# Post-norm, residual update and next pre-norm done by halves of the tokens, in a two-layer DeltaNet / RWKV-7 decoder step

## The chip, the cores and the metric

The kernel runs on one core of one Trainium2 chip. The metric is device time in microseconds (us) for one execution, as the median of three runs. TensorE is called PE here, VectorE DVE, ScalarE ACT, GpSimd POOL and the queue of SyncE, which issues all transfers, SP.

## The reference, cut to what matters

Two layers process 512 prompt tokens and 32 sample tokens (544 in all, width 1024). Each layer is a feed-forward block, a mixer, and a second feed-forward block, each of them between two RMS norms:

```
h = h + 0.5 * rms_norm(swiglu(rms_norm(h, ng[0]), w_in, w_out), ng[1])
u = rms_norm(h, ng[2])
out = gdn_mixer(u, ...)  if i % 2 == 0 else rwkv_mixer(u, ...)
h = h + rms_norm(out, ng[3])
h = h + 0.5 * rms_norm(swiglu(rms_norm(h, ng[4]), w_in2, w_out2), ng[5])
```

So six products end in a post-norm (norms 1, 3, 5, 7, 9, 11), and five of these are followed at once by the pre-norm of the next block (norms 2, 4, 6, 8, 10).

## The kernel before

Activations lie transposed: the 1024 features are 8 tiles `m` of 128 partitions, and each tile has 2 halves of `HALF` = 272 tokens. The residual is `h`, with row `2*m + half` of the tile. Products are done in fp32 precision by three matmuls of a split operand: weights are `whi + wlo`, activations `xh + xl` (or `mh + ml` inside a feed-forward block), and one product step is `xh*whi`, `xl*whi`, `xh*wlo`, each 128x128 weights by 272 tokens. A unit is one column tile of weights: `unit_mm` (L318) runs half 0 over all 8 row tiles (11 for the feed-forward outputs, which have two units per column tile), then half 1, and raises `acc` after each half. SP loads weights into four `raw` slots, ACT copies a slot to `whi` (`split_hi`, L277, and `early_hi`, L288), and POOL subtracts for `wlo` (`split_lo`, L302, and `early_lo`, L294).

At the end of an output product (`ffn0_out`, `gdn_out`, `ffn1_out`, `ffn2_out`, `wo`, `ffn3_out`) this happens for each column tile: ACT copies it to `y` with the norm's gain (L567) and squares it to `tb` (L570), and DVE adds up the squares in `tb[2]` (L587). During the last unit ACT already splits the first three units of the next product (`early_hi`, two into buffers of their own, the third into `whi`). After the last tile, `norm_pe` sums squares over the partitions with matmuls of a 128x32 block of ones (`quarter_sums`, L388, four blocks of 136 tokens), ACT takes the root (`norm_act`, L423), ACT splits unit 3 of the next product (`early_hi(..., 3)`, L288, with POOL's L294 behind it), DVE takes the reciprocal (`root_dve`, L431), and PE spreads the result to all partitions with an identity column (`spread_norm_pe`, L414).

Then `post_norm_dve` goes through the 8 tiles, whole tiles of 544 tokens: `tb[3] = y * row` (L476), `h += step * tb[3]` (L480), with the low part of the tile before, `xl = h*gain - xh` (`pre_norm_low`, L465), in between. ACT follows with `xh = h*gain` (L451) and the square (L455). PE takes each tile as it comes (`behind_norm_tiles`): units 0 and 1 in both halves, unit 2 in half 0 alone (its other half lies in a PSUM bank that holds the post-norm's row), and between unit 0 and unit 1 the tile's sum of squares for the pre-norm (`square_sum_pe`, L388). The products are L350 to L352. After the last tile come the other half of unit 2 (`behind_norm_half`), the spread of the pre-norm's root, and unit 3. The pre-norm's root scales the products afterwards, so PE doesn't wait for it before the first products.

Before norm 8 (`lora`) DVE also scales two weight tiles (`lora_scale_dve`), and ACT splits both unit 2 and unit 3 there after the root. All queues are written out by hand in program order, with semaphores between them. After the last block DVE updates 8 tiles, and SP stores two tiles at a time (`yT`).

Of the kernel before, what the change touches and what calls it, by code (L numbers as in the profile page):

```python
# [22 lines left out]
P = 128  # L23
# [45 lines left out]
for _name, _units, _kt in PRODUCTS:  # L69
# [10 lines left out]
SETS = {n: i for i, n in enumerate(  # L80
    ["ffn0_in", "gdn_in", "gdn_out", "ffn1_in", "ffn2_in", "lora", "x0", "x1", "x2", "wo", "ffn3_in"])}
# [47 lines left out]
def trunk_kernel(nc, a):  # L129

    es = ExitStack()
    with es:
# [185 lines left out]
        def unit_mm(pe, name, u, j, out, hi, lo, k0=0, start=True, stop=True, ready=None):  # L318
# [5 lines left out]
            for half in range(2):  # L324
                for k in range(kt):
                    if ready is not None and half == 0:
                        pe.wait_ge(x_lo, ready + k + 1)
                    wh = whi[two][:, k * P:(k + 1) * P]
                    wl = wlo[two][:, k * P:(k + 1) * P]
                    r = 2 * (k0 + k) + half  # L330
                    o = out[:, half, :]
                    pe.matmul(o, wh, hi[:, r, :], start=(start and k == 0), stop=False)  # L332
                    pe.matmul(o, wh, lo[:, r, :], start=False, stop=False)  # L333
                    mm = pe.matmul(o, wl, hi[:, r, :], start=False, stop=(stop and k == kt - 1))  # L334
                mm.then_inc(acc, 1)

        def first_units_mm(pe, name, sett):
# [3 lines left out]
            for k in range(NM):  # L341
                pe.wait_ge(x_lo, 8 * sett + k + 1)
# [13 lines left out]
        def behind_norm_mm(pe, name, q):  # L356
            behind_norm_tiles(pe, name, q)
            behind_norm_half(pe, name)
# [3 lines left out]
        def behind_norm_tiles(pe, name, q):  # L362
# [3 lines left out]
            for k in range(NM):  # L366
                pe.wait_ge(x_lo, 8 * SETS[name] + k + 1)
                for j in range(3):
                    if k == 0:
                        pe.wait_ge(w_lo, base + j + 1)  # L370
                    if j == 1:
                        square_sum_pe(pe, q, k)
                    first_products(pe, j, k, *bufs[j], halves=(0, 1) if j < 2 else (0,))
            if q:
                pe.wait_ge(h_upd, 8 * (q // 2))

        def behind_norm_half(pe, name):
            two = BASE[name] % 2
            for k in range(NM):
                first_products(pe, 2, k, whi[two], wlo[two], halves=(1,))  # L380


        QT = T // 4

        def quarter_sums(pe, bank, t, first, last):

            for qd in range(4):
                mm = pe.matmul(ps[32 * qd:32 * qd + 32, bank, HALF:HALF + QT], M["ones"][:, 0:32],  # L388
                               t[:, qd // 2, QT * (qd % 2):QT * (qd % 2) + QT], start=first, stop=last)
            return mm  # L390

        def post_rows():
            return ps[:, 5:7, 0:HALF]
# [4 lines left out]
        def square_sum_pe(pe, q, m):  # L398
            pe.wait_ge(sq_ready, 8 * q + m + 1)
            mm = quarter_sums(pe, norm_bank(q), tb[m % 2], m == 0, m == NM - 1)  # L400
            mm.then_inc(sq_added, 1)

        def post_sums_pe(pe, q):
            pe.wait_ge(sq_added, 8 * q + 7)
            pe.wait_ge(sq_ready, 8 * q + 8)
            quarter_sums(pe, norm_bank(q), tb[2], True, False)
            quarter_sums(pe, norm_bank(q), tb[1], False, True).then_inc(sq_added, 1)

        def spread_norm_pe(pe, q):

            pe.wait_ge(rs_ready, q + 1)
            for qd in range(4):
                o = ps[:, qd, HALF:HALF + QT] if q % 2 == 0 else post_rows()[:, qd // 2, QT * (qd % 2):QT * (qd % 2) + QT]
                mm = pe.matmul(o, M["ident"][:, 32 * qd:32 * qd + 1].broadcast_to([P, P]), rs[:, 0, 0:QT], start=True, stop=True)  # L414
            mm.then_inc(nrm_mm, 1)

        def norm_pe(pe, q):
            post_sums_pe(pe, q)
            spread_norm_pe(pe, q)

        def norm_act(act, q):
            act.wait_ge(sq_added, 8 * (q + 1))
            act.activation(rs[:, 0, 0:QT], ps[:, norm_bank(q), HALF:HALF + QT], ACT.Sqrt, bias=eps[:, 0:1], scale=1.0 / D).then_inc(rt_ready, 1)  # L423

        def norm_copy_act(act, q):
            act.wait_ge(nrm_mm, q + 1)
            act.activation(flat(rs).rearrange("p (q t) -> p q t", q=4), ps[:, 0:4, HALF:HALF + QT], ACT.Copy).then_inc(rs_full, 1)

        def root_dve(dve, q):
            dve.wait_ge(rt_ready, q + 1)  # L430
            dve.reciprocal(rs[:, 0, 0:QT], rs[:, 0, 0:QT]).then_inc(rs_ready, 1)  # L431

# [4 lines left out]
        def clear_squares(dve, q):  # L437

            dve.wait_ge(nrm_mm, q)
# [3 lines left out]
        def pre_norm_act(act, q, sett):  # L443

            for m in range(NM):
                if q:
                    act.wait_ge(h_upd, 8 * (q // 2 - 1) + m + 1)
                elif m % 2 == 0:
                    act.wait_ge(h_in[m // 2], 16)
                if sett is not None:  # L450
                    act.activation(xh[:, 2 * m:2 * m + 2, :], h[:, 2 * m:2 * m + 2, :], ACT.Copy,  # L451
                                   scale=v(V_NORM + q * NM + m)).then_inc(x_hi, 1)
                if 8 * q + m - 1 > 0:
                    act.wait_ge(sq_added, 8 * q + m - 1)
                act.activation(tb[m % 2][:, :, :], h[:, 2 * m:2 * m + 2, :], ACT.Square).then_inc(sq_ready, 1)  # L455
                if q == 0 and m == 5:
                    early_hi(act, "ffn0_in", 3)
            norm_act(act, q)
            if sett is None:
                norm_copy_act(act, q)  # L460

        def pre_norm_low(dve, q, sett, m):

            dve.wait_ge(x_hi, 8 * sett + m + 1)
            dve.scalar_tensor_tensor(xl[:, 2 * m:2 * m + 2, :], h[:, 2 * m:2 * m + 2, :], v(V_NORM + q * NM + m),  # L465
                                     xh[:, 2 * m:2 * m + 2, :].bitcast(F32), ALU.mult, ALU.subtract).then_inc(x_lo, 1)

        def post_norm_dve(dve, q, step, sett=None, y=y):

            root_dve(dve, q)  # L470
            dve.wait_ge(nrm_mm, q + 1)
            base = 8 * (q // 2)
            for m in range(NM):
                if base + m > 0:
                    dve.wait_ge(h_upd, base + m)
                dve.tensor_tensor(tb[3][:, :, :], y[:, 2 * m:2 * m + 2, :], post_rows(), ALU.mult).then_inc(h_tmp, 1)  # L476
                if sett is not None and m:
                    pre_norm_low(dve, q + 1, sett, m - 1)
                dve.wait_ge(h_tmp, base + m + 1)
                dve.scalar_tensor_tensor(h[:, 2 * m:2 * m + 2, :], tb[3][:, :, :], step,  # L480
                                         h[:, 2 * m:2 * m + 2, :], ALU.mult, ALU.add).then_inc(h_upd, 1)
            if sett is not None:
                pre_norm_low(dve, q + 1, sett, NM - 1)


        def ffn_pe(pe, f):
# [11 lines left out]
            def out_body(i, first):  # L498
                for j in range(4):
                    m2 = j // 2  # L500
                    if j % 2 == 0 and not first:
                        pe.wait_ge(sq_ready, 8 * q + 2 * i + m2 - 1)
# [4 lines left out]
                    unit_mm(pe, name, i * 4, j, pair(m2), mh, ml, k0=KTO * (j % 2), start=(j % 2 == 0), stop=(j % 2 == 1))  # L507
            out_body(0, True)
            with pe.Fori(1, 4) as i:
                out_body(i, False)  # L510
# [34 lines left out]
        def out_act(act, name, per_tile, q, then, y=y, begun=False, ahead=0):  # L545
# [6 lines left out]
            def body(i, last):  # L552
                for j in range(4):
# [8 lines left out]
                    if j % per_tile == per_tile - 1:  # L562
                        mt = j // per_tile
                        m = (4 // per_tile) * i + mt
                        act.wait_ge(acc, 2 * (n + 1))

                        act.activation(y[:, ds(2 * m, 2), :], pair(mt), ACT.Copy, scale=vec[:, ds(V_NORM + q * NM + m, 1)])  # L567
                        if not isinstance(i, int) or i or mt >= 2:
                            act.wait_ge(sq_added, 8 * q + m - 1)
# [9 lines left out]
        def out_dve(dve, name, per_tile, q):  # L579
            clear_squares(dve, q)  # L580

            def body(i, last):
                for mt in range(4 // per_tile - last):
                    m = (4 // per_tile) * i + mt
                    dve.wait_ge(sq_ready, 8 * q + m + 1)
                    dve.wait_ge(sq_added, 8 * q + m)
# [2438 lines left out]
```

## Time and profile before

| | |
|---|---|
| runs | 2829.35, 2828.2, 2829.18 us; median 2829.18 us |
| profiled execution | span of 2825.6 us from its first to its last instruction; the record gives no separate time for it, the median is 3.6 us above this span |
| busy | PE 93%, DVE 40%, POOL 37%, ACT 31% |
| mean granted PE clock | 0.962 of 2.4 GHz |
| chain that ended last | PE, nearly throughout |
| DMA | 202.8 MB, 72 GB/s mean |

How to read it: an engine's busy time is the union of its instructions; matmuls are pipelined, so the start of one and the start of the next give what one costs PE, and its own duration (0.29 us for a product of 272 tokens at full clock) is longer than that. A bracket behind a row tells how long the engine was idle before it, and what ended the idle time.

### The profile page before, as it was taken

What the parts mean: (1) busy time and instruction counts of PE and PEld (TensorE: products, weight loads), DVE (VectorE), ACT (ScalarE), POOL (GpSimd) and SP (SyncE); (2) the same over time, 40 slices, a digit from 0 to 9 for tenths busy, and PEclk for the clock granted to TensorE, in tenths of its full rate; (3) what the DMA queues carried; (4) which work ended last, traced back from release to release, by engine and by line L of the source; (5) the groups of instructions that cost most, each with busy time, mean ns of one, the idle gap of its engine ahead of it and who ended that gap; (6) DMA issues with size and microseconds to landing.
All of it is one profiled execution on the core that took longest, in us unless ns stands there. A gap on an engine that the chain in (4) does not pass through costs nothing. (4 is left out here: it accounts for less than half of the span.)

```text
span 2825.6 us, 61605 instructions
## 1 busy us (share of the span) xinstructions
PE 2623.7 (93%) x26993; PEld 2540.6 (90%) x26993; DVE 1124.5 (40%) x1382; ACT 880.2 (31%) x1223; POOL 1056.0 (37%) x495
## 2 busy tenths in 40 slices
PE   7999998997999999999999999799588888999997
PEld 7999998996888899999899999799377858999997
DVE  3333117845544433321433311631654454433312
ACT  4222223233323422222322222333523333322221
POOL 3444442333434344443344443133034353244432
PEclk9999999998998999999999999899789999999999
DMA  4223221221012222322222222122000022122221
GB/s 149 82 89 99 92 74 60 87 67 38 2 61 105 68 89 82 94 93 81 62 88 89 92 92 85 32 89 73 19 3 3 4 81 81 53 89 89 99 88 46
DMA packets 53585, 202.82 MB, mean 72 GB/s; under 512 B 6320, under 2 KB 6448, under 8 KB 53424
## 3 DMA queue, kind: packets, MB, share of 16 engines
q1 hardware_dynamic: 53424, 200.38, 21.7%
q8 instruction: 137, 2.24, 0.3%
q14 instruction: 24, 0.20, 0.0%
HBM read 190.68 MB, written 9.67 MB: 71 GB/s over the span
## 5 line engine op out<-in xcount | busy, mean ns | idle before, releaser
L302 POOL TENSOR_TENSOR wlo<-raw,whi 128x1024 fp32r<-128x1024 f32 (+1 forms) x261 | 708.8, 2716 | 1124.8 <-ACT whi L277 1124.8
L332 PE MATMUL ps<-xh,whi 128*128 128x272 f32 x3600 | 1039.5, 289 | 6.6 <-POOL wlo L302 3.2
L334 PE MATMUL ps<-xh,wlo 128*128 128x272 f32 x3600 | 1043.5, 290 | 0.0
L333 PE MATMUL ps<-xl,whi 128*128 128x272 f32 x3600 | 1036.0, 288 | 0.0
L332 PEld LDWEIGHTS ps<-xh,whi 128*128 128x128 f32 x3600 | 678.6, 189 | 9.8 <-issue 5.8
L333 PEld LDWEIGHTS ps<-xl,whi 128*128 128x128 f32 x3600 | 679.5, 189 | 0.0
L334 PEld LDWEIGHTS ps<-xh,wlo 128*128 128x128 f32 x3600 | 677.4, 188 | 0.0
L277 ACT ACTIVATE whi<-raw 128x1024 fp32r<-128x1024 f32 (+1 forms) x261 | 297.7, 1140 | 1128.3 <-PE ps L334 1108.4
L334 PE MATMUL ps<-mh,wlo 128*128 128x272 f32 x1408 | 406.1, 288 | 0.0
L333 PE MATMUL ps<-ml,whi 128*128 128x272 f32 x1408 | 405.4, 288 | 0.0
L332 PE MATMUL ps<-mh,whi 128*128 128x272 f32 x1408 | 405.0, 288 | 0.0
L587 DVE TENSOR_TENSOR tb<-tb,tb 128x544 f32<-128x544 f32 x42 | 100.5, 2393 | 430.6 <-ACT tb L570 430.5
L333 PEld LDWEIGHTS ps<-ml,whi 128*128 128x128 f32 x1408 | 265.1, 188 | 0.0
L332 PEld LDWEIGHTS ps<-mh,whi 128*128 128x128 f32 x1408 | 265.0, 188 | 0.0
L334 PEld LDWEIGHTS ps<-mh,wlo 128*128 128x128 f32 x1408 | 264.4, 188 | 0.0
L604 DVE TENSOR_TENSOR tb<-ps,rs 128x544 f32<-128x544 f32 x88 | 63.7, 724 | 426.7 <-PE ps L334 426.7
L609 DVE TENSOR_TENSOR ml<-tb,mh 128x544 f32 x88 | 166.3, 1890 | 84.8 <-ACT mh L537 84.8
L602 DVE TENSOR_TENSOR tb<-ps,rs 128x544 f32<-128x544 f32 x88 | 63.8, 725 | 148.3 <-PE ps L334 129.3
L1871 POOL TENSOR_TENSOR wlo<-raw,whi 128x1024 fp32r<-128x1024 f32 x18 | 44.9, 2497 | 112.9 <-ACT whi L1864 112.9
L2468 POOL TENSOR_TENSOR sZL<-sZ,cmask 128x512 f32<-128x512 f32 x48 | 56.3, 1194 | 61.6 <-PE ps L2199 35.3
L537 ACT ACTIVATE mh<-tb 128x544 f32 (+1 forms) x88 | 58.2, 661 | 52.8 <-DVE tb L607 52.3
L607 DVE TENSOR_TENSOR tb<-tb,tb 128x544 f32<-128x544 f32 x88 | 63.9, 727 | 10.4 <-ACT tb L534 1.7
(470 smaller groups left out, 3295.2 us busy)
## 6 DMA issues: line engine op xcount, KB each, us to landing
raw<-w SPq DMA_DIRECT2D x245, 512.0 KB, 3.5
raw<-w SPq DMA_DIRECT2D x64, 704.0 KB, 4.1
mS<-state_gdn SPq DMA_DIRECT2D x8, 512.0 KB, 5.0
gdn_s_s<-mS SPq DMA_DIRECT2D x8, 512.0 KB, 2.8
h<-xT SPq DMA_DIRECT2D x4, 544.0 KB, 8.0
yT<-h SPq DMA_DIRECT2D x4, 544.0 KB, 2.7
go_r<-w SPq DMA_DIRECT2D x4, 512.0 KB, 5.6
S<-state_rwkv SPq DMA_DIRECT2D x8, 256.0 KB, 4.1
```

Of the source, the lines that this page charges most:

```text
L277: act.activation(whi[two][:, 0:kt * P], raw[slot][:, 0:kt * P], ACT.Copy).then_inc(w_hi, 1)
L302: pool.tensor_tensor(wlo[two][:, 0:kt * P], raw[slot][:, 0:kt * P], whi[two][:, 0:kt * P].bitcast(F32), ALU.subtract).then_inc(w_lo, 1)
L332: pe.matmul(o, wh, hi[:, r, :], start=(start and k == 0), stop=False)
L333: pe.matmul(o, wh, lo[:, r, :], start=False, stop=False)
L334: mm = pe.matmul(o, wl, hi[:, r, :], start=False, stop=(stop and k == kt - 1))
L537: act.activation(mh[:, ds(2 * jj, 2), :], tb[2 + j // 2][:, :, :], ACT.Copy).then_inc(mid_hi, 1)
L587: dve.tensor_tensor(tb[2][:, :, :], tb[2][:, :, :], tb[mt % 2][:, :, :], ALU.add).then_inc(sq_added, 1)
L602: dve.tensor_tensor(tb[two][:, :, :], pair(2 * two), rs[:, :, :], ALU.mult).then_inc(gate_scaled, 1)
L604: dve.tensor_tensor(tb[2 + two][:, :, :], pair(2 * two + 1), rs[:, :, :], ALU.mult).then_inc(up_scaled, 1)
L607: dve.tensor_tensor(tb[2 + two][:, :, :], tb[two][:, :, :], tb[2 + two][:, :, :], ALU.mult).then_inc(mult_done, 1)
L609: dve.tensor_tensor(ml[:, ds(2 * jj, 2), :], tb[2 + two][:, :, :], mh[:, ds(2 * jj, 2), :].bitcast(F32), ALU.subtract).then_inc(mid_lo, 1)
L2468: pool.tensor_tensor(zl[g][:, :, :], Zb[g][:, :, :], cmask[:, l, :].unsqueeze(1).broadcast_to([P, 8, 64]), ALU.mult).then_inc(W["zl"], 1)
```

## The change

The post-norm's last tile, its sums, root, reciprocal and spread go by halves of the tokens. In the last unit of an output product, which is written out after a shortened loop, `unit_mm` gets a function `between` that is called in half 1: after 3 row tiles it issues half 0's sums, after 9 (7 in the mixers' outputs) half 0's spread. ACT squares half 0 of the last tile as soon as that half is done, then copies it, then takes the root, and then does the same for half 1. DVE updates `h` for half 0 of all tiles (in groups of 1, 1, 2, 2, 2 tiles), then for half 1 (four groups of 2). `pre_norm_act` and `pre_norm_low` go by half tiles, and `behind_norm_tiles` runs half 0 of units 0, 1 and 2 over all tiles, then half 1; sums of squares come once per half tile. The spread for half 1 stands behind the third half tile. In the first norm (q = 0) ACT, DVE and the sums work on whole tiles as before, but PE takes the halves in turn there too. In `lora` a small subtraction (`shift_low_dve`) moves from in front of the post-norm into its second half, and the carried products of unit 2 move in front of the last half tile. The stores of `yT` become 8 of half the size. `SETS` and other counts change from eight per set to running totals.

```diff
-        def unit_mm(pe, name, u, j, out, hi, lo, k0=0, start=True, stop=True, ready=None):
+        def unit_mm(pe, name, u, j, out, hi, lo, k0=0, start=True, stop=True, between=None):
...
+                    if between is not None and half == 1:
+                        between(k)
...
+            for hf in range(2):
+                for k in range(NM):
+                    if q or hf == 0:
+                        pe.wait_ge(x_lo, SETS[name] + NM * hf + k + 1)
+                    if hf and k == 0 and q:
+                        pe.wait_ge(h_upd, UPDATES * (q // 2 - 1) + len(TILE_GROUPS[0]))
+                    if hf and k == NM - 1 and inside is not None:
+                        inside()
+                    for j in range(3):
...
+                        if j == 1 and q:
+                            square_sum_pe(pe, q, k, hf)
...
+                        first_products(pe, j, k, *bufs[j], halves=(hf,))
+                    if q and hf == 0 and k == 2:
+                        spread_post_pe(pe, q - 1, 1)
...
+        ET = T // 8
+        TILE_GROUPS = (((0,), (1,), (2, 3), (4, 5), (6, 7)), ((0, 1), (2, 3), (4, 5), (6, 7)))
...
+        def part_sums(pe, bank, t, hf, first, last):
             for qd in range(4):
+                mm = pe.matmul(ps[32 * qd:32 * qd + 32, bank, HALF + ET * hf:HALF + ET * hf + ET], M["ones"][:, 0:32],
+                               t[:, hf, ET * qd:ET * qd + ET], start=first, stop=last)
...
+        def post_sums_pe(pe, q, hf):
+            pe.wait_ge(sq_added, squares_before(q) + 7)
+            pe.wait_ge(sq_ready, squares_before(q) + 8 + hf)
+            part_sums(pe, norm_bank(q), tb[2], hf, True, False)
+            part_sums(pe, norm_bank(q), tb[1], hf, False, True).then_inc(sq_added, 1)
...
+        def spread_post_pe(pe, q, hf):
+            pe.wait_ge(rs_ready, norms_before(q) + hf + 1)
+            for qd in range(4):
+                mm = pe.matmul(post_row(hf)[:, ET * qd:ET * qd + ET], M["ident"][:, 32 * qd:32 * qd + 1].broadcast_to([P, P]),
+                               rs[:, 0, ET * hf:ET * hf + ET], start=True, stop=True)
+            mm.then_inc(nrm_mm, 1)
...
+        def pre_norm_act(act, q):
+            for hf in range(2):
+                for m in range(NM):
+                    act.wait_ge(h_upd, UPDATES * (q // 2 - 1) + update_of(m, hf) + 1)
+                    act.activation(xh[:, 2 * m + hf, :], h[:, 2 * m + hf, :], ACT.Copy, scale=v(V_NORM + q * NM + m)).then_inc(x_hi, 1)
+                    act.wait_ge(sq_added, squares_before(q) + NM * hf + m - 1)
+                    act.activation(tb[m % 2][:, hf, :], h[:, 2 * m + hf, :], ACT.Square).then_inc(sq_ready, 1)
             norm_act(act, q)
...
+        def post_norm_dve(dve, q, step, sett=None, y=y, inside=None):
+            base = UPDATES * (q // 2)
+            root_post_dve(dve, q, 0)
+            lows = []
+            for hf in range(2):
+                dve.wait_ge(nrm_mm, norms_before(q) + hf + 1)
+                for i, ms in enumerate(TILE_GROUPS[hf]):
+                    n = base + update_of(ms[0], hf)
+                    tmp_ = tb[3][:, 0:len(ms), :]
+                    if n > 0:
+                        dve.wait_ge(h_upd, n)
+                    dve.tensor_tensor(tmp_, of_half(y, ms, hf), post_row(hf).unsqueeze(1).broadcast_to([P, len(ms), HALF]),
+                                      ALU.mult).then_inc(h_tmp, 1)
+                    if hf == 0 and i == 1:
+                        root_post_dve(dve, q, 1)
+                    if hf and i == 0 and inside is not None:
+                        inside()
+                    while lows:
+                        pre_norm_low(dve, q + 1, sett, *lows.pop(0))
+                    dve.wait_ge(h_tmp, n + 1)
+                    dve.scalar_tensor_tensor(of_half(h, ms, hf), tmp_, step, of_half(h, ms, hf), ALU.mult, ALU.add).then_inc(h_upd, 1)
+                    if sett is not None:
+                        lows += [(m, hf) for m in ms]
...
+            out_body(0, True, False)
+            with pe.Fori(1, 3) as i:
+                out_body(i, False, False)
+            out_body(3, False, True)
+            post_sums_pe(pe, q, 1)
...
+                        if last and j == 3:
+                            for hf in range(2):
+                                act.wait_ge(acc, 2 * n + 1 + hf)
+                                act.wait_ge(sq_added, squares_before(q) + m - 1)
+                                act.activation(tb[1][:, hf, :], pair(mt)[:, hf, :], ACT.Square).then_inc(sq_ready, 1)
+                                act.activation(y[:, 2 * m + hf, :], pair(mt)[:, hf, :], ACT.Copy, scale=v(V_NORM + q * NM + m))
+                                root_post_act(act, q, hf)
+                            continue
...
+            for hf in range(2):
+                for i in range(4):
+                    sp.wait_ge(h_upd, UPDATES * 5 + update_of(2 * i + 1, hf) + 1)
+                    sp.dma_start(h_half(a["yT"], i, hf), h_half(h, i, hf)).then_inc(out_done, 16)
```

## Rows read from the trace of the kernel before

**Rows 1.** The page's first line.
```profile
span 2825.6 us, 61605 instructions
```
**Rows 2.** Timeline, ffn0_out to gdn_in: start us, us, engine, line, out<-in, count.
```profile
419.74 0.28 PE L333 MATMUL ps<-ml,whi 128*128 128x272 f32 x1
419.87 0.29 PE L334 MATMUL ps<-mh,wlo 128*128 128x272 f32 x1
421.56 0.67 PE L388 MATMUL ps<-tb,mf 128*32 128x136 f32 x16 [1.41 <-ACT tb L570]
...
428.58 0.60 PE L350 MATMUL ps<-xh,gdn_in_eh 128*128 128x272 f32 x1 [3.17 <-DVE xl L465]
...
422.56 1.05 ACT L288 ACTIVATE whi<-raw 128x1024 fp32r<-128x1024 f32 x1
...
423.69 2.36 POOL L294 TENSOR_TENSOR wlo<-raw,whi 128x1024 fp32r<-128x1024 f32 x1 [3.43 <-ACT whi L288]
```
**Rows 3.** Timeline, same boundary: the last tile's sum, the pre-norm's root, its spread.
```profile
449.05 0.29 PE L352 MATMUL ps<-xh,gdn_in_el 128*128 128x272 f32 x1
449.27 0.44 PE L388 MATMUL ps<-tb,mf 128*32 128x136 f32 x8
449.64 0.39 PE L350 MATMUL ps<-xh,gdn_in_eh 128*128 128x272 f32 x1
...
450.18 1.00 DVE L431 RECIPROCAL rs<-rs 128x136 f32<-128x136 f32 x1 [5.63 <-ACT rs L423]
...
453.90 1.09 PE L414 MATMUL ps<-rs,mf 128*128 128x136 f32 x8
454.74 0.37 PE L332 MATMUL ps<-xh,whi 128*128 128x272 f32 x1
```
**Rows 4.** Stretches: engines busy (x instructions), then PEclk, DMA share, GB/s.
```profile
432.50:434.50 2.00, 2.00 (x10) 1.79 (x8) 1.90 (x4) 0.98 (x2) 0.00 (x0) 0.50 0.00 0
434.50:436.50 2.00, 2.00 (x21) 1.74 (x21) 1.97 (x3) 1.25 (x2) 0.00 (x0) 0.98 0.00 0
```
**Rows 5.** Timeline at gdn_out to ffn1_in, then ffn2_out to lora.
```profile
930.97 1.05 ACT L288 ACTIVATE whi<-raw 128x1024 fp32r<-128x1024 f32 x1
...
933.58 0.29 PE L334 MATMUL ps<-xh,wlo 128*128 128x272 f32 x1
...
942.83 0.59 PE L350 MATMUL ps<-xh,ffn_in_eh 128*128 128x272 f32 x1 [3.17 <-DVE xl L465]
...
1763.29 0.29 PE L334 MATMUL ps<-mh,wlo 128*128 128x272 f32 x1
...
1775.88 0.60 PE L350 MATMUL ps<-xh,lora_eh 128*128 128x272 f32 x1 [3.18 <-DVE xl L465]
...
1768.16 1.40 DVE L1942 TENSOR_TENSOR sh_l<-shin,sh_h 128x64 fp32r<-128x64 f32 x1 [11.44 <-ACT sh_h L1973]
```
**Rows 6.** Timeline inside wo: a POOL split and a DVE sum at once.
```profile
2361.60 2.43 POOL L302 TENSOR_TENSOR wlo<-raw,whi 128x1024 fp32r<-128x1024 f32 x1 [4.74 <-ACT whi L277]
...
2362.67 1.94 DVE L587 TENSOR_TENSOR tb<-tb,tb 128x544 f32<-128x544 f32 x1 [5.24 <-ACT tb L570]
```
**Rows 7.** Small operations: groups by line (busy, mean ns, idle), then the timeline.
```profile
L841 DVE TENSOR_TENSOR ext<-ps,rs 128x272 f32<-128x272 f32 x24 | 10.3, 430 | 0.0
...
1797.25 0.25 PE L2005 MATMUL ps<-sh_h,wlo 128*128 128x8 f32 x1
1797.36 0.25 PE L2003 MATMUL ps<-sh_h,whi 128*128 128x8 f32 x1
```
**Rows 8.** Chain that ended last (start us, us), and the page's store of yT.
```profile
2805.60 0.71 ACT y L567
...
2810.40 0.73 DVE tb L476
...
2821.75 0.73 DVE h L480
...
yT<-h SPq DMA_DIRECT2D x4, 544.0 KB, 2.7
```

More of the change, by code:

```diff
@@ L78 @@
 N8, N11 = _n8, _n11
-SETS = {n: i for i, n in enumerate(
-    ["ffn0_in", "gdn_in", "gdn_out", "ffn1_in", "ffn2_in", "lora", "x0", "x1", "x2", "wo", "ffn3_in"])}
+SETS, _sets = {}, 0
+for _name, _parts in (("ffn0_in", NM), ("gdn_in", 2 * NM), ("gdn_out", NM), ("ffn1_in", 2 * NM), ("ffn2_in", 2 * NM), ("lora", 2 * NM),
+                      ("x0", NM), ("x1", NM), ("x2", NM), ("wo", NM), ("ffn3_in", 2 * NM)):
+    SETS[_name] = _sets
+    _sets += _parts
 def masks():
@@ L377, in behind_norm_half @@
[L377 to L380, printed above, removed]
-        QT = T // 4
-        def quarter_sums(pe, bank, t, first, last):
+            for hf in range(2):
[7 more added lines that the diff above has]
+                    for j in range(3):
+                        if hf == 0 and k == 0:
+                            pe.wait_ge(w_lo, base + j + 1)
+                        if j == 1 and q:
+                            square_sum_pe(pe, q, k, hf)
+                        elif j == 1 and hf == 0:
+                            square_sum_pe(pe, q, k, None)
+                        first_products(pe, j, k, *bufs[j], halves=(hf,))
+                    if q and hf == 0 and k == 2:
+                        spread_post_pe(pe, q - 1, 1)
@@ L468, in post_norm_dve @@
[L468 to L483, printed above, removed]
+            norm_act(act, 0)
@@ L506, in out_body, with post_between, between @@
                         pe.wait_ge(mid_lo, nb + NF)
[L507 to L510, printed above, removed]
+                    unit_mm(pe, name, i * 4, j, pair(m2), mh, ml, k0=KTO * (j % 2), start=(j % 2 == 0), stop=(j % 2 == 1),
+                            between=post_between(pe, q, 3, 9) if last and j == 3 else None)
+            out_body(0, True, False)
[3 more added lines that the diff above has]
+            post_sums_pe(pe, q, 1)
+        def post_between(pe, q, sums_at, spread_at):
+            def between(k):
+                if k == sums_at:
+                    post_sums_pe(pe, q, 0)
+                if k == spread_at:
+                    spread_post_pe(pe, q, 0)
+            return between
         FFN_NORM = [0, 4, 6, 10]
@@ L2938, in _ @@
             ffn_pe(pe, 0)
-            norm_pe(pe, 1)
             gdn_pe(pe)
```

180 lines of the change are left out of this document (87 added, 93 removed).

## The prediction

> **What bounds the kernel.** I read the page first, then the chain that ended last, then the timeline of each engine at the six places where an output product meets the next block, and the stretches there for PE's clock. The span is 2825.6 us [rows 1], and the chain lies on PE almost throughout: whatever PE does not do in a stretch is lost, and whatever is added to PE's queue there is added to the time. The change touches five meetings of blocks and the end; the rest is untouched.
>
> One meeting, ffn0_out to gdn_in, shows the pattern. Products start 0.125 us apart (one takes 419.74 to 419.87), so PE has issued its last product by E = 420.0 and starts the next at 428.58 [rows 2]: a gap of 8.6 us, with the post-norm's sums in it and its spread. From there to unit 3 at 454.74 [rows 3] PE never runs out of work, but is not all products: units 0 to 2 are 144 products, 18.1 us. A tile's sum costs more than it looks: the product at 449.05 would have been followed at 449.18; the sum starts at 449.27, the next product at 449.64, and this first one is 0.10 longer than others (0.39 for 0.29), so 0.57 us, and 8 of them 4.5. The spread from 453.90 to 454.74 and the long product behind it cost 0.92 [rows 3]. PE also runs at half clock until about 434.5: 0.50 in one stretch, 0.98 in the next [rows 4], that is 6.0 us of running at half speed, 3.0 lost. 8.6 + 18.1 + 4.5 + 0.9 + 3.0 = 35.1, against 34.7 from E to unit 3: the account closes within 0.4.
>
> ffn1_out to ffn2_in looks the same. Behind gdn_out the gap is 9.1 (933.58 + 0.13 to 942.83), behind wo likewise; at lora it is 12.5 (1763.42 to 1775.88), because DVE's small subtraction is held up until 1769.56 and the reciprocal is queued behind it [rows 5].
>
> **The change, part by part** (us on PE's path, per meeting; + is slower).
>
> *Before E.* Half 0's sums and spread now stand between products of the last unit. The sums are two tiles (16 instructions, 0.67 for 0.44 of one tile [rows 2, 3]): 0.57 + 0.23 less a shorter end, 0.74. The spread at half the columns I price at its full 0.92, because products with only 8 columns still start 0.11 apart (1797.25, 1797.36 [rows 7]), and 8 of those are 0.89; the lower bound is half, 0.46. So E moves to E' = E + 1.66. The spread's wait is covered: root and reciprocal take about 1.6 us after the sums, and 12 to 18 products (1.5 to 2.3) stand between.
>
> *The gap.* DVE can start half 0 about half a microsecond before E', but it is not DVE that decides. ACT squares half 1, PE sums it (before: sums 1.56 after E behind a whole tile's copy and square; now half a square, I take 0.8 after E'), then ACT takes the root and splits unit 3, in program order ahead of the first `xh`. Before, this split began 1.00 after the sums (422.56), and POOL's part ran from 423.69 to 426.05 [rows 2], done before DVE's updates began. Now ACT's split begins at E' + 1.8, POOL's runs from 2.9 to 5.3, and the first `xh` is ready at about 3.4, in the middle of it. The first `xl` has two SBUF operands, like DVE's sum at 2362.67: that began 1.07 after a POOL split of 2.43, should take 0.73, and ended 0.58 after POOL did [rows 6]. So DVE waits for POOL, ends 0.3 behind it (a half tile: 0.43 [rows 7] in place of 0.72), and PE starts at E' + 5.6. Without the hold-up it would be 3.8, the lower bound. Gap against before: 1.66 + 5.6 - 8.6 = -1.3; behind gdn_out and wo, ACT ends its early splits only at 932.02 [rows 5], after half 0 of the last unit (3.0 before E), which holds up the sums 0.7 inside the unit: 1.66 + 0.7 + 5.6 - 9.1 = -1.1.
>
> *Sums by halves.* 16 sums in place of 8. All bookkeeping (wait, change of weights, restart) stays; only columns are halved. Bounds: 0.57 each if nothing shrinks, 0.28 if all does. By the 8-column row, short matmuls are paced by something other than columns, so I take off only the last round's 68 columns twice, 0.06: 0.51. 16 x 0.51 - 4.5 = +3.7.
>
> The Trainium skill, "TensorE: Matmul & The Clock Gate", section "Back-to-back issue gap", puts the spacing of matmuls on a running array down to the moving columns; by that alone the sums would halve and the time would be rival 2's. The same page's section on LDWEIGHTS makes a weight load go by weight columns, unchanged here; the trace's 0.11 at 8 columns sides with that one.
>
> *Spread for half 1* behind the third half tile: +0.92 (lower bound 0.46).
>
> *The pre-norm's root.* Before, 24 products of unit 2 (3.0 us) stood behind the last sum and hid root and reciprocal (449.27 to 451.18 [rows 3]). Now 6 do: the sum ends its cost at +0.4, the products at +1.1, the root is there at +1.9. PE waits 0.8 (bounds 0 and 1.2). In lora 24 tiny products (2.7) still hide it: 0.
>
> *Half tiles on DVE and ACT.* Two half tiles take DVE some 2.3 us (two operations of 0.73 [rows 8] over the pair, two `xl` of 0.43), PE 2 x (9 products + sum) = 3.3: PE stays the pace, as it does before, when a tile takes it 15 products and a sum, 2.45. The updates cost nothing as long as that holds; if not, it is under 1 per meeting.
>
> Sum: after ffn0_out and ffn1_out -1.3 + 3.7 + 0.9 + 0.8 = +4.1 each; after gdn_out and wo +4.3 each; lora: 1.66 + 5.6 - 12.5 = -5.2, + 3.7 + 0.9, and 1.0 because two splits now stand on POOL there and the second holds up the second half tile: +0.4. Together +17.2. The half-clock stretch I leave as it is: PE idles 4.2 on end in the new gap, long enough by the old one's pattern.
>
> *The first norm.* Tiles 6 and 7's `xl` meet POOL's split of unit 3 [rows 6], and PE, with 9 products a tile in place of 15 while it waits for tiles, gets there sooner: +0.7 (0 to 1.5).
>
> *The end.* Before, DVE starts 2810.40, 5.0 after E, and ends at 2822.5 [rows 8]. Now it starts at E' - 0.5 (2806.6), updates one half tile and multiplies the next (1.3), waits for half 1's root until E' + 2.3 = 2809.4, and has 0.45 and seven pairs of 1.5 left: 2820.4, so -2.1. Half 1's spread is long there by then. The last store is half as large; 2.7 [rows 8] falls by an estimated 0.7. Together -2.8. Four more stores on SP delay nothing, since none waits behind them.
>
> Loop peeling, counters and reordering on ACT: nothing; PE runs other unrolled stretches at the same 0.125, and ACT has the whole unit as cover.
>
> Total: 17.2 + 0.7 - 2.8 = +15. The profiled execution's span would be 2841, and the median, 3.6 above the span, 2844.
>
> **The rivals.**
> 1. *Clock.* PE's longest idle stretch shrinks from the old gap of 8.6 to about 4.2, and PE's clock may not fall at all. At most 3.0 come back per meeting, 15 in all: 2829, no change. Against it: the clock had already fallen when the old gap ended, and sums and spread inside that gap did not hold it up.
> 2. *The inserts go by columns* (the other side). If a half sum costs 0.28 and a half spread 0.46, each meeting saves 16 x 0.23 + 2 x 0.46 + 0.4 = 5.0, in all 25: 2819, faster. It decides from a half sum of about 0.32 downwards. For it: columns are all that changes per matmul. Against it: the 8-column spacing, and that sums show 0.1 of idle before and a slow product after.
> 3. *POOL does not hold up DVE*, because the order or a free port lets `xl` through: 1.8 less per meeting, 9 in all: 2835, at the edge of measurable.
>
> **How the numbers follow.** 0.2% is 5.7 us, about what a measurement of this kernel can tell from no change. Forecast as worked out 0.58; clock 0.14; columns 0.10; no hold-up 0.18. The first gives slower, clock gives same, columns faster, and hold-up falls half to slower, half to same; I take 0.01 off slower for a mixture of the last three: slower 0.66, same 0.23, faster 0.11. The forecast's own range is 2836 to 2850: a sum at 0.57 adds 5, spreads at half take off 5, starvation at the first half tiles adds 1 to 2. The range for 8 in 10 leaves out the columns case and what lies above: 2827 to 2851.
>
> **What would show it.** Right: the first L350 some 7 us after the last L334 without inserts, with POOL's last early split ending just before it; 16 sums per pre-norm at about 0.5 each; PE waiting some 0.8 for DVE's reciprocal before the pre-norm's spread; the tail from the last product to the end shorter by about 4 than before. Wrong: half clock gone behind the meetings, sums at 0.3, or DVE's first `xl` done while POOL runs.

## Result and the profile after

The changed kernel takes 2839.24 us (median of five runs, 2838.37 to 2845.39), the kernel before 2828.20 (five runs beside it, 2823.15 to 2829.35): a ratio of 1.0045, with a 95% interval of 1.0033 to 1.0057, or 12.7 us slower (9.3 to 16.1). The forecast was 2844, slower, with 2836 to 2850 as its own range.

The profiled execution of the changed kernel was the longest of its five. Its page's first line stands against the one in [rows 1]:

```profile
span 2843.5 us, 62712 instructions
```

The timeline of the changed kernel answers to [rows 2] and [rows 3] line by line. (Products are now L335 to L337 in units and L353 to L355 in the stream; post-norm and pre-norm sums L411; spreads L450 and L442; `xl` is L518, the update of `h` L546, the splits of early units L291 on ACT and L297 on POOL.) First lines from the first norm, then the meeting of ffn0_out and gdn_in and the end of its stream; then two lines from lora and the last product of all.

```profile
26.38 2.43 POOL L297 TENSOR_TENSOR wlo<-raw,whi 128x1024 fp32r<-128x1024 f32 x1 [12.40 <-ACT whi L291]
26.98 4.31 DVE L512 SCALAR_TENSOR_TENSOR xl<-h,vec,xh 128x544 fp32r<-128x544 f32 x2 [1.86 <-ACT xh L491]
27.59 0.44 PE L425 MATMUL ps<-tb,mf 128*32 128x136 f32 x8
29.44 0.39 PE L353 MATMUL ps<-xh,ffn_in_eh 128*128 128x272 f32 x1 [0.46 <-DVE xl L512]
30.01 0.44 PE L425 MATMUL ps<-tb,mf 128*32 128x136 f32 x8
31.92 0.44 PE L425 MATMUL ps<-tb,mf 128*32 128x136 f32 x8
...
420.45 0.45 PE L411 MATMUL ps<-tb,mf 128*32 128x68 f32 x16
...
423.18 1.01 PE L450 MATMUL ps<-rs,mf 128*128 128x68 f32 x8
...
424.70 0.28 PE L337 MATMUL ps<-mh,wlo 128*128 128x272 f32 x1
...
425.56 0.45 PE L411 MATMUL ps<-tb,mf 128*32 128x68 f32 x16 [0.58 <-ACT tb L648]
...
426.28 1.05 ACT L291 ACTIVATE whi<-raw 128x1024 fp32r<-128x1024 f32 x1
...
427.41 2.34 POOL L297 TENSOR_TENSOR wlo<-raw,whi 128x1024 fp32r<-128x1024 f32 x1 [3.79 <-ACT whi L291]
...
427.77 2.27 DVE L518 SCALAR_TENSOR_TENSOR xl<-h,vec,xh 128x272 fp32r<-128x272 f32 x1 [0.78 <-ACT xh L504]
...
430.10 0.59 PE L353 MATMUL ps<-xh,gdn_in_eh 128*128 128x272 f32 x1 [4.09 <-DVE xl L518]
...
430.49 0.43 PE L354 MATMUL ps<-xl,gdn_in_eh 128*128 128x272 f32 x1
...
430.72 0.43 PE L355 MATMUL ps<-xh,gdn_in_el 128*128 128x272 f32 x1
...
455.75 0.33 PE L411 MATMUL ps<-tb,mf 128*32 128x68 f32 x8
...
457.33 0.33 PE L411 MATMUL ps<-tb,mf 128*32 128x68 f32 x8
458.13 1.00 DVE L465 RECIPROCAL rs<-rs 128x136 f32<-128x136 f32 x1 [3.77 <-ACT rs L456]
459.28 1.16 PE L442 MATMUL ps<-rs,mf 128*128 128x136 f32 x8 [0.67 <-DVE rs L465]
460.19 0.38 PE L335 MATMUL ps<-xh,whi 128*128 128x272 f32 x1
...
1776.57 4.88 POOL L297 TENSOR_TENSOR wlo<-raw,whi 128x1024 fp32r<-128x1024 f32 x2 [6.17 <-ACT whi L291]
...
1779.14 2.61 DVE L546 SCALAR_TENSOR_TENSOR h<-tb,h 128x272 f32<-128x272 f32 x1
...
2827.65 0.28 PE L337 MATMUL ps<-mh,wlo 128*128 128x272 f32 x1
```

What to see in it. Half 0's sums and spread now stand ahead of the last product at 424.70. From there to the first product of the stream PE is without products for 430.10 - 424.83 = 5.28 us; it was 8.6 [rows 2]. What ends the wait is an `xl` of half a tile that takes 2.27 us, and it ends 0.3 behind POOL's split of unit 3. In the stream a sum recurs after 1.58 us (455.75 to 457.33); less nine products at 0.125 that is 0.45 for a half sum. At the end PE waits 0.67 for the reciprocal, and unit 3 starts 35.5 after the last product of the block before, 0.6 later than it did [rows 2, 3], with the inserts (0.57 for two tiles' half sums, 0.89 for the spread) not yet counted.

The list of all waits shows that each meeting does the same: the first wait below falls on five first products and lora's second half tile, the second on the pre-norm's spread in all meetings but lora's (engine, line, what it waited for: us in total, times, longest).

```profile
PE ps L353 <- DVE xl L518: 21.1, 6, 4.1
...
PE ps L442 <- DVE rs L465: 2.7, 4, 0.7
```

Behind the gap the clock falls as it did [rows 4]: in stretches (busy time of each engine, then PEclk, DMA share and GB/s) it is at half, 0.50, and back at full by 436. At half clock (1.2 of 2.4 GHz) products start 0.23 us apart (430.49, 430.72) and not 0.125, so that each us at half clock costs PE about 0.45. The last two rows are lora's stream, from its first product to unit 3, in the kernel before and then in the kernel after: 33.00 us at a granted clock of 0.86, and 40.33 at 0.80. That is 9 us at half clock against 16.

```profile
427.00:430.00 3.00, 0.00 (x0) 0.00 (x0) 2.23 (x2) 1.06 (x3) 2.34 (x1) 0.70 0.85 288
430.00:433.00 3.00, 2.90 (x18) 2.46 (x19) 2.93 (x7) 1.60 (x5) 0.00 (x0) 0.50 0.97 370
433.00:436.00 3.00, 3.00 (x29) 2.42 (x28) 2.64 (x5) 1.38 (x4) 0.00 (x0) 0.66 0.20 81
...
1775.88:1808.88 33.00, 33.00 (x265) 29.81 (x265) 15.23 (x21) 12.73 (x19) 4.74 (x2) 0.86 0.01 3
...
1779.27:1819.60 40.33, 39.72 (x336) 34.77 (x337) 20.11 (x32) 16.40 (x35) 6.87 (x3) 0.80 0.13 41
```

### The profile page after: what moved, and what is told of

The parts are those of the page before. It is cut to its first block and busy times, and to the rows that moved or that the text cites. A ratio compares the mean times of both kernels' runs of the same rounds, so it can differ in the third digit from the quotient of the medians.

```text
span 2843.5 us, 62712 instructions
## 1 busy us (share of the span) xinstructions
PE 2652.7 (93%) x27457; PEld 2561.4 (90%) x27457; DVE 1138.5 (40%) x1440; ACT 899.2 (32%) x1321; POOL 1055.5 (37%) x495
## 5 line engine op out<-in xcount | busy, mean ns | idle before, releaser
L335 PE MATMUL ps<-xh,whi 128*128 128x272 f32 x3600 | 1039.8, 289 | 4.2 <-POOL wlo L305 2.3
L337 PE MATMUL ps<-xh,wlo 128*128 128x272 f32 x3600 | 1043.4, 290 | 0.0
L335 PEld LDWEIGHTS ps<-xh,whi 128*128 128x128 f32 x3600 | 678.6, 188 | 7.6 <-issue 4.9
L337 PEld LDWEIGHTS ps<-xh,wlo 128*128 128x128 f32 x3600 | 677.5, 188 | 0.0
L337 PE MATMUL ps<-mh,wlo 128*128 128x272 f32 x1408 | 406.1, 288 | 0.0
L335 PE MATMUL ps<-mh,whi 128*128 128x272 f32 x1408 | 405.8, 288 | 0.0
L674 DVE TENSOR_TENSOR tb<-tb,tb 128x544 f32<-128x544 f32 x42 | 100.4, 2390 | 430.7 <-ACT tb L657 430.6
L335 PEld LDWEIGHTS ps<-mh,whi 128*128 128x128 f32 x1408 | 265.0, 188 | 0.4
L337 PEld LDWEIGHTS ps<-mh,wlo 128*128 128x128 f32 x1408 | 264.5, 188 | 0.0
L353 PE MATMUL ps<-xh,ffn_in_eh 128*128 128x272 f32 x128 | 46.9, 366 | 28.7 <-DMA mf<-mf 15.9
```

The costliest lines, as they stand in the source:

```text
L353: pe.matmul(o, wh, xh[:, r, :], start=(k == 0), stop=False)
L674: dve.tensor_tensor(tb[2][:, :, :], tb[2][:, :, :], tb[mt % 2][:, :, :], ALU.add).then_inc(sq_added, 1)
```

## The experiments

Two theories stood at the start. The prediction's own: the half sums, the half spreads and the uncovered root are costs of PE, POOL's split of unit 3 sets the gap, and only the program's end gains. Against it: the clock, or the pace of DVE, decides, so that single costs taken away come back elsewhere. Each ratio below is against the kernel before on the same chip; the kernel after stands at 1.0045. For every run the quantity that I follow in the trace is the time from the start of a block's last product to the start of unit 3 in the next, without inserts ahead of it. Lora's meeting is left out, and run 7 (the kernel before but for its end) stands in as a second execution of the old meetings, run 4 as one of the new. In the last column each us at half clock between the first product and unit 3 is taken out at 0.45:

```
last product to unit 3, us       gdn_in  ffn1_in  ffn2_in  ffn3_in   mean   less half clock
before                            34.87    34.45    34.82    34.77   34.73   32.4
the end alone (run 7)             33.50    34.93    33.70    34.79   34.23   32.3
after                             35.49    35.96    35.40    36.18   35.76   33.3
first norm as before (run 4)      35.23    35.66    35.22    36.05   35.54   33.3
unit 3's split late               32.11    32.84    33.41    32.89   32.81   30.9
unit 2's half 1 last              34.31    34.71    34.69    34.03   34.44   32.4
whole sums                        32.80    33.48    32.52    32.07   32.72   30.7
four edits together               28.62    29.63    28.61    29.72   29.15   27.6
no overlap                        37.34    37.95    36.96    37.87   37.53   35.4
no overlap, split late            35.38    34.85    35.55    35.46   35.31   33.2
```

The last column is needed because one meeting of the same code differs by up to 1.4 us from one execution to the next, as its stream meets the half clock for longer or shorter. Here is gdn_in's, from the first product to unit 3, in the kernel before and in run 7:

```profile
428.58:454.74 26.16, 26.16 (x217) 22.85 (x217) 15.21 (x21) 10.38 (x16) 0.00 (x0) 0.89 0.03 11
...
430.36:455.40 25.04, 25.04 (x217) 21.84 (x217) 15.22 (x21) 10.33 (x16) 0.00 (x0) 0.93 0.05 18
```

With the half clock taken out, the four meetings of the kernel after and those of run 4 lie within 0.05 us of each other.

**1. Unit 3's split late.** The split leaves the head of the meeting (in `pre_ffn_act`, and likewise ahead of gdn_in and lora) for `pre_norm_act`; GpSimd follows ScalarE by itself.

```diff
-            early_hi(act, f"ffn{f}_in", 3)
...
                     act.activation(xh[:, 2 * m + hf, :], ...).then_inc(x_hi, 1)
+                    if hf and m == (3 if name == "lora" else NM - 1):
+                        early_hi(act, name, 3)
```

> Edit: in the meetings before gdn_in, ffn1_in, ffn2_in and ffn3_in ScalarE's high part of unit 3's weights, and with it GpSimd's low part, moves from the head of the meeting to just before the last square of half 1; in the one before lora to half 1's fourth tile (unit 2's split stays at the head there). Theory: GpSimd's 2.3 us split stretches the first correction of half 0 from 0.5 to 2.27, so it sets the first product behind the meeting; without it the gap of 5.3 us comes to about 3.6 in four meetings, -1.7 each, about 2832. Rival A: the stream behind the gap takes up the time again (VectorE's corrections or the half clock pace it), 2839. Rival B: with a gap this short the granted clock doesn't fall either, some 3 us more in each of the four, about 2820.

Measured: 2821.68 us, ratio 0.9980 (0.9971 to 0.9988), 0.65% or some 18 us under the kernel after. Its timeline at the same meeting:

```profile
424.39 0.28 PE L337 MATMUL ps<-mh,wlo 128*128 128x272 f32 x1
...
425.97 0.51 ACT L504 ACTIVATE xh<-h,vec 128x272 fp32r<-128x272 f32 x1
...
426.60 0.42 DVE L520 SCALAR_TENSOR_TENSOR xl<-h,vec,xh 128x272 fp32r<-128x272 f32 x1
...
427.07 0.40 PE L353 MATMUL ps<-xh,gdn_in_eh 128*128 128x272 f32 x1 [1.37 <-DVE xl L520]
...
451.16 2.43 POOL L297 TENSOR_TENSOR wlo<-raw,whi 128x1024 fp32r<-128x1024 f32 x1 [27.86 <-ACT whi L291]
```

The same `xl` takes 0.42 us without POOL beside it and 2.27 with it: the hold-up is shown, and the split is in time for unit 3 from its new place. The gap is 2.56 here and in ffn2_in, 3.24 to 3.27 in the other two. That is 2.0 to 2.7 less, not 1.7, since ScalarE's own part of the split (1.05) also stood ahead of the first `xh`. Behind the mixers it is 3.3 and not 2.56 because there another split, unit 2's, is still on POOL and holds up the first update of `h` (0.44 elsewhere), which again ends 0.3 behind it:

```profile
931.70 2.39 POOL L297 TENSOR_TENSOR wlo<-raw,whi 128x1024 fp32r<-128x1024 f32 x1
...
932.70 1.70 DVE L548 SCALAR_TENSOR_TENSOR h<-tb,h 128x272 f32<-128x272 f32 x1
```

In lora, where unit 2's split stays at the head by this edit, the gap stays too (5.27). The meetings themselves are shorter by 3.0 on the average, and by 2.3 with the half clock taken out, which is what the gaps lost. Rival B holds only in part: the clock still falls in all four, but over the stream from the first product to unit 3 it is 0.94 in three of them, where after has 0.90 to 0.92; in ffn2_in, behind the same gap of 2.56, it is 0.90. In gdn_in's:

```profile
427.00:430.00 3.00, 2.93 (x19) 2.57 (x20) 2.93 (x7) 1.64 (x5) 0.00 (x0) 0.59 0.76 257
430.00:433.00 3.00, 3.00 (x32) 2.32 (x31) 2.61 (x5) 1.84 (x6) 0.00 (x0) 0.84 0.62 250
```

Four meetings at 3.0 are 12 of the 18 us. The rest I don't place with certainty: lora's stream is about 1 shorter there, and the remaining 5 are no more than the interval of the two ratios.

**2. Unit 2's half 1 behind the last sum.**

```diff
-                    for j in range(3):
+                    for j in range(2 if hf and q else 3):
...
             if q:
+                for k in range(NM):
+                    first_products(pe, 2, k, *bufs[2], halves=(1,))
```

> Edit: unit 2's products on half 1 leave the stream and stand behind the last square's sum, ahead of the spread of the pre-norm, as in the kernel before; the half stream and all sums stay. Theory: 8 x 3 products (3 us) cover root and reciprocal, the wait of about 0.7 us on the reciprocal ahead of the spread goes in four meetings: -2.8, about 2836.5. Rival: the stream of half 1, now six products and a sum for each tile (1.2 us), comes to wait for ScalarE's squares or VectorE's corrections, and loses there what the root gave: 2839.

Measured: 2835.53 us, ratio 1.0029 (1.0019 to 1.0040): 4.5 us under the kernel after, intervals overlapping. In the timeline (of gdn_in) the spread follows the last product with no wait:

```profile
454.36 1.00 DVE L467 RECIPROCAL rs<-rs 128x136 f32<-128x136 f32 x1 [2.53 <-ACT rs L458]
...
457.17 0.29 PE L355 MATMUL ps<-xh,wlo 128*128 128x272 f32 x1
457.30 1.09 PE L444 MATMUL ps<-rs,mf 128*128 128x136 f32 x8
```

The reciprocal is done nearly 2 us before the products end, so the 0.67 is gone, as the theory has it. The meetings are shorter by 1.3 on the average, 0.9 with the half clock taken out, of which the root is 0.67; the last 0.2 I don't place. Gaps are unchanged at 5.27 to 5.30.

**3. Whole sums.** The squares of both halves of a tile are taken and added at once, while half 1 is streamed.

```diff
-                        if j == 1 and q:
-                            square_sum_pe(pe, q, k, hf)
-                        elif j == 1 and hf == 0:
+                        if j == 1 and hf == (q > 0):
                             square_sum_pe(pe, q, k, None)
...
-                    act.activation(tb[m % 2][:, hf, :], h[:, 2 * m + hf, :], ACT.Square)...
+                    if hf:
...
+                        act.activation(tb[m % 2][:, :, :], h[:, 2 * m:2 * m + 2, :], ACT.Square)...
```

> Edit: the pre-norm's squares and their sums are made once for each whole tile, during half 1; half 0 has products alone: 8 sums for each meeting and not 16. Theory: a sum costs PE some 0.45 us at half the columns and 0.57 at all, so 16 x 0.45 - 8 x 0.57 = 2.6 us in each of five meetings if PE bounds both halves: -13, about 2826. Between: half 0 then runs at VectorE's pace (about 1.25 us for each tile by its three operations, not PE's 1.13), 1.6 each, about 2831. Rival (sums go by columns and cost about 0.28 each, or are hidden in the stream): no change within 2 us, 2838 to 2840.

Measured: 2826.15 us, ratio 0.9987 (0.9976 to 0.9997), 16 us under the kernel after and no slower than before. In the timeline the last two sums of the stream:

```profile
452.59 0.44 PE L423 MATMUL ps<-tb,mf 128*32 128x136 f32 x8
454.29 0.44 PE L423 MATMUL ps<-tb,mf 128*32 128x136 f32 x8
```

1.70 from sum to sum, less nine products at 0.125, is 0.57 for a whole sum, where a half sum was 0.45: half the columns saved a fifth. The meetings are 3.0 shorter, 2.6 with the half clock taken out, as expected. The doubled number of sums is the largest of the costs that the change puts on PE's own queue, and it is paid for the number of matmuls more than for their columns.

**4. The first norm as before** (whole tiles for units 0 and 1, unit 2's half 1 behind the sums, for `q == 0` alone).

```diff
+            if q == 0:
+                for k in range(NM):
...
+                    for j in range(3):
...
+                        if j == 1:
+                            square_sum_pe(pe, q, k, None)
+                        first_products(pe, j, k, *bufs[j], halves=(0, 1) if j < 2 else (0,))
+                for k in range(NM):
+                    first_products(pe, 2, k, *bufs[2], halves=(1,))
+                return
```

> Edit: the first norm of the program (there is no post-norm ahead of it) takes the three units' products in the order of the kernel before, whole tiles for units 0 and 1, and unit 2's half 1 behind the sums; all else as in the kernel after. Theory of the prediction: the new order costs 0.7 us there (root not hidden). Read from the profile: first product to unit 3's start was 25.1 us before. Rival: it costs about 2 us, of which more than the root is a wait for the tiles of h in the stream, since half 0's three products for each tile need the tiles faster than they come in; then this run's stretch is some 2 us shorter than after's and the wait inside the stream is gone.

Measured: one execution, 2832.41 us. First product to unit 3 is 24.97 us, against 27.06 in the kernel after. Over all profiles of this study the old order takes 24.97 to 25.76 (four profiles, before's among them) and the new one 25.91 to 27.28 (six), medians 1.6 apart. Two things make up the 1.6. The first is the wait for the last tiles of `h`. In the kernel after, tile 6's sum comes 2.42 behind tile 5's and tile 7's 1.91 behind that (27.59, 30.01, 31.92), where nine products and a sum take 1.70, because POOL's split at 26.38, and a cast of a mask right behind it (28.75, 1.96), hold up the two `xl`: 4.31 for both, where one takes 0.79 elsewhere. That is 0.9 us, alike in all six profiles of the new order and in none of the old. It is what the prediction priced at 0.7; its 0.7 was for this meeting of POOL and DVE and not for the root, as the expectation above has it. The rest is the clock: the first products of the program start 0.23 apart, as at half clock (PEclk is no guide there, its record begins later), and 0.125 apart only from 3.5 us behind the first one in run 4 and from 6.1 in the kernel after; 2.6 us at 0.45 are 1.2. So of the 2.1 between these two profiles the order costs 0.9.

**5. The four edits in one kernel.**

> Edit: the four edits of the runs before in one kernel (unit 3's split late, unit 2's half 1 behind the last sum, one sum for each whole tile, the first norm in the old order). Theory: they are separate costs of PE and add up: by their ratios 1.0045 - 0.0065 - 0.0016 - 0.0058 - 0.0007 (the last from one profile, 2 us) = 0.990, about 2799. Rival: VectorE's three operations for a tile (about 1.25 us) set the pace as soon as PE's tile on a half costs less (1.13 us in half 0, 1.3 in half 1), so that only about half of the two streams' gains is left: 0.994, about 2809.

Measured: 2804.64 us, ratio 0.9921 (0.9908 to 0.9933): faster than both kernels, by 22 us than before and by 35 than after. The single edits take 2.95, 1.32 and 3.04 from a meeting, together 7.3; in one kernel it is 6.6. The 0.7 is the clock: with the half clock taken out the three take 2.3, 0.9 and 2.6, and the one kernel 5.7. So they add up, and DVE's pace is no bound. In the timeline, gap and sums:

```profile
426.46 0.40 PE L353 MATMUL ps<-xh,gdn_in_eh 128*128 128x272 f32 x1 [1.37 <-DVE xl L533]
...
441.13 0.44 PE L437 MATMUL ps<-tb,mf 128*32 128x136 f32 x8
...
442.44 0.44 PE L437 MATMUL ps<-tb,mf 128*32 128x136 f32 x8
```

A tile of half 1 takes 1.31: six products and a sum at 0.57, PE's own pace.

**6. No overlap**, and **8. no overlap with unit 3's split late**. In the five meetings half 0's sum and spread go behind the last product; run 8 has run 1's edit besides. The diff is that of `ffn_pe`; `out_pe`, for gdn_out and wo, is edited alike.

```diff
-                            between=post_between(pe, q, 3, 9) if last and j == 3 else None)
+                            between=post_between(pe, q, 3, 9) if last and j == 3 and f == 3 else None)
...
+            if f < 3:
+                post_sums_pe(pe, q, 0)
             post_sums_pe(pe, q, 1)
+            if f < 3:
+                spread_post_pe(pe, q, 0)
```

> Edit: in the five meetings half 0's sum and spread are not put between the last unit's products but stand behind them (half sums, half spreads and the stream by halves stay as in the kernel after; the end of the program too). Theory: after's 5.3 us gap is set by GpSimd's split of unit 3, which starts only once ScalarE has the last root, so norming half 0 early brings little: last product to first product 6.7 us with the two inserts now, about 7.2 without overlap; +0.5 in each of five meetings, 1.0045 + 0.0009, about 2842. Rival: the overlap is worth the whole chain of sum, root, reciprocal and spread, some 3.5 us less the two inserts of 1.5: +2 in each, 1.008, about 2850.

> Edit: as the run without overlap, with unit 3's split late as well. Theory: with GpSimd out of the way the chain through sum, root, reciprocal and spread decides; last product to first product about 5.7 us, where with overlap and a late split it was 2.6 to 3.3 and 1.5 of inserts: +1.3 in each of five meetings over the run with unit 3's split late (0.998), 1.0003, about 2827. Rival: the overlap is worth nothing here either, since the stream behind is paced by the half clock and VectorE: 0.998.

Measured: 6 takes 2837.83 us, ratio 1.0038 (1.0025 to 1.0051), not to be told from after; 8 takes 2825.88, ratio 1.0003 (0.9995 to 1.0012), 0.23% above run 1 where 0.23% was expected (that the two agree so closely is luck: with the half clock taken out, the four meetings and lora's gap give some 3 us of these 6.5). The timeline of 6:

```profile
422.60 0.29 PE L337 MATMUL ps<-mh,wlo 128*128 128x272 f32 x1
...
425.92 2.35 POOL L297 TENSOR_TENSOR wlo<-raw,whi 128x1024 fp32r<-128x1024 f32 x1 [2.92 <-ACT whi L291]
426.07 2.50 DVE L546 SCALAR_TENSOR_TENSOR h<-tb,h 128x272 f32<-128x272 f32 x1
...
429.90 0.60 PE L353 MATMUL ps<-xh,gdn_in_eh 128*128 128x272 f32 x1 [4.34 <-DVE xl L518]
```

and of 8:

```profile
422.15 0.29 PE L337 MATMUL ps<-mh,wlo 128*128 128x272 f32 x1
...
425.62 0.44 DVE L548 SCALAR_TENSOR_TENSOR h<-tb,h 128x272 f32<-128x272 f32 x1
...
427.40 0.60 PE L353 MATMUL ps<-xh,gdn_in_eh 128*128 128x272 f32 x1 [2.29 <-DVE xl L520]
```

In 6 the split meets the first update of `h` (2.50 for 0.44) instead of the first `xl`, and PE is without products for 7.17; after's 5.28 and its two inserts are 6.74. So in the changed kernel the norming of half 0 under the last unit, its central idea, gives 0.4 in that meeting and nothing that the time shows: over four meetings it is 37.5 either way, inserts and stalls included, and 0.4 less with the overlap when the half clock is taken out. At lora the gap is 8.5 without overlap against 5.28 and 1.46 with it, 1.7. With POOL out of the way the same step is worth more behind the feed-forward blocks: 5.12 without overlap, 2.56 and 1.46 of inserts with it, 1.1 in gdn_in and in ffn2_in alike. Behind the mixers it is worth nothing even then: 5.27 and 5.30 without it, and with it 3.27 and 3.24 of gap, 1.46 of inserts and 0.5 of stall, since unit 2's split holds up DVE there (run 1).

**7. The end alone**, in the kernel before: only the last norm and the store go by halves (same edits as in the change, for `q == 11`).

> Edit: the kernel before with only the program's last norm and store by halves as in the kernel after; the five meetings and the first norm as before. Theory of the prediction: -2.8 for the end, ratio 0.9990, about 2825. Rival: the eight smaller stores end no sooner and the inserts of 1.5 us eat what VectorE's start gives: no difference, 1.000.

Measured: 2821.37 us, ratio 0.9986 (0.9977 to 0.9995), 4.0 us faster (1.4 to 6.5). From the last product to the end of the span it is 15.7 us here and 15.7 in the kernel after (2843.5 less 2827.78); before it was 20.2. Less the inserts of 1.5 that is 3.0, for the 2.8 of the prediction.

## Why the prediction was right, point by point

```
term, us                               predicted   measured      less half clock
two tiles' half sums before E             0.74        0.57
half 0's spread                           0.92        0.89
E' to first product                       5.6         5.3
a half sum                                0.51        0.45
16 half sums less 8 whole ones           +3.7        +2.6
PE's wait for the pre-norm's root         0.8         0.7
ffn0_out, ffn1_out: whole meeting        +4.1        +2.1, +2.0    +2.6, +2.7
gdn_out, wo                              +4.3        +3.5, +3.4    +2.5, +2.5
lora                                     +0.4        +1.6          -1.7
first norm                               +0.7        +1.6          +0.9
end                                      -2.8        -3.0          -3.0
sum                                       +15         +11           +6.5
```

(Measured meetings: the table above, after less before, plus 1.46 of inserts, and 0.5 of stall on ScalarE behind gdn_out and wo; lora's two are 45.6 before and 45.7 after, with 9.1 and 16.4 us at half clock in them.) The sum of 11 stands against 12.7 (9.3 to 16.1) by the ratio of the runs, 11.0 by the medians.

The direction and the main terms were right for the reasons given, but the number is nearer than the terms deserve. With the half clock taken out the change costs some 6.5 us by these rows and not 15: each of the four meetings came out 1.4 to 1.8 cheaper than priced (half sums 1.1, gap and inserts 0.5, root 0.1), and lora 2.1 cheaper. The clock, put at nothing, gives the other 4.7 in these two profiles, 3.3 of them at lora. Two errors that partly cancel left the time inside the range; that is luck. Besides, the forecast adds 3.6 us from span to median, while all five executions of the kernel after lie 1.8 to 1.9 above their own span: the 3.6 came from comparing two executions of the kernel before.

- *The gap* was right in mechanism and nearly in size: ACT's split of unit 3, then POOL's, then the `xl` that waits for it. Run 1 shows POOL as the cause, and run 6, where the same split meets the update of `h` instead and stretches that, bears it out. The Trainium skill, "SBUF — State Buffer", section "Who interferes with whom", calls the ports that DVE shares with GpSimd an exclusive lock; 0.42 against 2.27 for one `xl` agrees.
- *The half sums* were mis-sized by 0.06 each, 1.0 a meeting: columns count for a little more than the last round. Rival 2 needed 0.32 or less; 0.45 lies about midway between that and the whole sum's 0.57. Run 3 shows the price by taking half of the sums away.
- *The spreads* cost their full price at half the columns, as priced.
- *The root* was right, and run 2 takes the wait away.
- *lora* was mis-sized. The second split does hold up the second half tile (the update at 1779.14 takes 2.61, and PE waits 0.6), but with the half clock taken out the meeting still comes out 1.7 shorter, and the clock takes it back. PE stays at half clock for 7.4 us from its first product; before, products were back at 0.125 after 3.6 us. Later in the stream the clock falls once more, for 9 us up to unit 3 against 5.5 before. That is 7.3 us more at half clock, 3.3 lost. Run 4, with the same code there, has 16.5 us at half clock too, and run 7, with the old code, 9.1; runs 2, 5 and 8, which edit that code, have 12.1, 7.0 and 9.5. What makes the difference no run here shows. The prediction left the half-clock stretch as it is for all five.
- *The first norm* was right in mechanism and size, 0.9 for 0.7; the profiles' 1.6 has the clock in it (run 4).
- *The rivals*: the clock fell again, even in run 1, so rival 1 did not hold; POOL did hold up DVE, so rival 3 did not; and a half sum at 0.45 leaves rival 2 out.

## What to carry to other kernels

Work done early is worth only what the next wait on the same path leaves of it: here a 2.3 us operation on POOL, queued by ACT behind the last root, took most of the gain of norming half the tokens ahead of the end (0.4 left of 1.1), and moving that one operation gave it back where no other split stood on POOL. Cutting a chain of short matmuls in half doubles a price that hardly depends on their size, so go by halves where latency is waited for (the post-norm) and by whole tiles where only throughput counts (the pre-norm's sums). And keep something behind the last sum that covers the root. When single profiles are compared, take out the time at half clock first: here it was as large as the differences looked for.

## What the runs showed of the hardware

A sum at half its columns (68 for 136) costs PE 0.45 us for 0.57, a spread at half its columns 0.89 for 0.92. A DVE operation with two SBUF operands on half a tile that met a POOL split ended 0.3 us behind the split, whether the split had 1.4 us left to run (run 1, `h`: 1.70 for 0.44) or 2.0 (after, `xl`: 2.27 for 0.42). After a gap of only 2.56 us PE still shows half clock. How long it stays there does not go by the gap alone: behind 2.56 the streams of gdn_in and ffn2_in ran at a granted clock of 0.94 and 0.90 in one execution of run 1, and gdn_in's, in the same code, at 0.89 and 0.93 behind gaps of 8.6 and 8.3 (before, run 7).

Stretches that no edit touches differ from one execution to the next: from the reciprocal of lora's pre-norm to wo's last product, the same code in the kernel after and in runs 1, 3 and 4, the profiles show 597.9, 589.9, 597.7 and 591.1 us. The clock accounts for most of it: 111, 93, 108 and 97 us of these are at half clock, and at 0.45 for each what is left is 547.8, 548.1, 549.2 and 547.3. The kernel after's profiled execution, the longest of its five, has such a long stretch; so its span lies 17.9 above before's while the medians are 11.0 apart, and the sums above are made by stretch.
